# Moving VectorE's rotation of block one's q and k by a chunk, and reordering block two's feature chunks

## The reference

```python
def first_block(x, ...):                  # block one
    z = rmsnorm(x, g) @ w_in              # attention q, k, v | rwkv columns | gates
    q, k = rope(z_q), rope(z_k)           # 3 groups x 4 heads x 64, rotated
    o_attn = dilated_attention(q, k, v)
    o_rwkv = rwkv7_time_mix(z_rwkv)       # a recurrence, done here as chains of small products
    ...
def second_block(h, ...):                 # block two
    p = split(rmsnorm(h) @ w_in_2)        # q_a k_a v_a q_b k_b v_b q_idx k_idx w_idx q_c k_cmp v_cmp ...
    o_b = dsa(rope(q_b), rope(k_b), v_b, rope(q_idx), rope(k_idx), w_idx)
    o_c = nsa(rope(q_c), rope(k_cmp), v_cmp, rope(k_sel), v_sel, rope(k_win), v_win, ...)
    ...
def _compress(tok, pos_emb, w1, w2):      # of k_cmp and of v_cmp
    return gelu(blocks(tok + pos_emb) @ w1) @ w2
```

## Time and profile before

| what | value |
|---|---|
| time, median of 3 runs | 909.61 us (909.11 to 909.75) |
| the profiled execution: its own time | 909.91 us |
| its span, first to last instruction | 907.4 us |
| TensorE busy / VectorE busy / ScalarE busy | 882.2 / 606.8 / 480.5 us |
| mean granted TensorE clock | 0.998 of full |

### The profile page before, as it was taken

How to read it: one execution, slowest core, us unless ns; L and a number is a source line. 1 busy time by engine, 2 the same in 40 slices (tenths; PEclk the granted TensorE clock), 3 DMA queues, 4 the chain that set the end, 5 groups by cost and what they waited for, 6 DMA issues and landing times.

```text
span 907.4 us, 15435 instructions
## 1 busy us (share of the span) xinstructions
PE 882.2 (97%) x6552; PEld 748.8 (83%) x6552; DVE 606.8 (67%) x976; ACT 480.5 (53%) x775; POOL 29.2 (3%) x51
## 2 busy tenths in 40 slices
PE   7999999999899999999999999999999999999997
PEld 4999898787689888888889978776788788888885
DVE  4578978557856666656766577877863566666673
ACT  4775667436534444456444856484622545555561
POOL 0010000010000000000000020000000000000000
PEclk9999999999999999999999999999999999999999
DMA  9644333224468665555339764353817566665521
GB/s 336 190 140 140 99 119 114 63 83 150 178 248 282 188 190 190 200 202 187 121 112 229 164 210 144 111 186 107 277 38 206 146 187 188 191 193 194 199 95 47
DMA packets 131204, 150.71 MB, mean 166 GB/s; under 512 B 11808, under 2 KB 102176, under 8 KB 131008
## 3 DMA queue, kind: packets, MB, share of 16 engines
q1 hardware_dynamic: 129920, 145.57, 51.8%
q10 hardware_dynamic: 1216, 4.16, 1.2%
HBM read 148.67 MB, written 1.05 MB: 165 GB/s over the span
## 4 chain that ended last, share of the span: by engine, by line
PE 85%; DVE 7%; ACT 4%; issue 2%; DMA 1%; POOL 0%; POOLq 0%; ACTq 0%; DVEq 0%
PE psum L821 12%; PE psum L716 9%; PE psum L718 9%; PE psum L717 9%; PE psum L826 7%; PE psum L774 4%; PE psum L794 3%; PE psum L795 3%; PE psum L803 3%; PE psum L722 3%; PE psum L870 2%; PE psum L880 2%; PE psum L871 2%; PE psum L827 2%; DVE parts L2705 2%
## 5 line engine op out<-in xcount | busy, mean ns | idle before, releaser
L1808 ACT ACTIVATE parts<-low 128x1024 fp32r<-128x1024 f32 (+3 forms) x252 | 254.3, 1044 | 65.6 <-PE psum L718 48.3
L2705 DVE TENSOR_TENSOR parts<-low,parts 128x1024 fp32r<-128x1024 f32 (+3 forms) x156 | 183.7, 1206 | 37.7 <-ACT parts L1808 37.5
L716 PE MATMUL psum<-parts 128*128 128x512 f32 (+2 forms) x424 | 169.1, 399 | 4.6 <-DVE parts L2705 2.5
L718 PE MATMUL psum<-parts 128*128 128x512 f32 (+2 forms) x424 | 163.5, 386 | 0.0
L717 PE MATMUL psum<-parts 128*128 128x512 f32 (+2 forms) x424 | 163.4, 385 | 0.0
L1808 ACT ACTIVATE high<-psum 128x512 f32<-128x512 f32 (+6 forms) x115 | 63.4, 560 | 134.2 <-PE psum L827 76.4
L821 PE MATMUL psum<-parts 128*128 128x512 f32 x462 | 116.8, 392 | 0.0
L716 PEld LDWEIGHTS psum<-parts 128*128 128x128 f32 x424 | 79.6, 188 | 26.3 <-DVE parts L2705 4.5
L821 PEld LDWEIGHTS psum<-parts 128*128 128x128 f32 x462 | 86.9, 188 | 16.9
L718 PEld LDWEIGHTS psum<-parts 128*128 128x128 f32 x424 | 79.6, 188 | 16.4
L717 PEld LDWEIGHTS psum<-parts 128*128 128x128 f32 x424 | 79.8, 188 | 13.9
(11 more groups left out here) (313 smaller groups left out, 1310.6 us busy)
## 6 DMA issues: line engine op xcount, KB each, us to landing
low<-in_w_in_dram SPq DMA_DIRECT2D x40, 1024.0 KB, 5.3
low<-in_w_ffn_in_dram SPq DMA_DIRECT2D x44, 512.0 KB, 5.2
low<-in_w_ff_in_dram SPq DMA_DIRECT2D x16, 1024.0 KB, 5.7
low<-in_w_ff_out_dram SPq DMA_DIRECT2D x16, 1024.0 KB, 4.8
low<-in_w_ffn_out_dram SPq DMA_DIRECT2D x11, 1024.0 KB, 5.0
low<-in_w_out_dram SPq DMA_DIRECT2D x8, 1024.0 KB, 5.2
low<-in_w_ple_gate_dram SPq DMA_DIRECT2D x4, 1024.0 KB, 5.0
low<-consts_dram ACTq DMA_DIRECT2D x1, 2078.0 KB, 9.0
```

Of the source, the lines that this page charges most:

```text
L716: mm(o, l[0], r[0], start, False)
L718: return mm(o, l[1], r[0], False, stop)
L1808: return e.activation(o, a, ACT.Copy)
L2705: tt(rslot3(n, nk, width)[:, r, 0:w], slot3(n, nk, width)[:, r, 0:w], st.hi3(j)[:, r, 0:w].bitcast(F32), ALU.subtract) \
```

## The change

There are five edits. (1) Block one: the rotations are given to chunks by a table. Chunk 1's step holds none, chunk 2's rotates chunk 0, chunk 3's rotates 1, chunk 4's rotates 2 and 3, chunk 5's rotates 4; `rope1(5)` stays in the first gate. The buffers `zs` are four, and ScalarE waits for the rotation four chunks back. (2) Block two: the gathered chunk is n = 2 and the short one n = 3; q_b, q_idx and q_c are n = 4 to 6. Waits on rotations name the new numbers, and the three key copies come behind chunk 4. (3) `ahead` is gone: every slot is split in the order of the chunks. (4) The token chunk of v writes banks 5 and 6. (5) The partial sums of `_compress` are added by one matmul per half with a constant that has a one wherever row and column agree modulo 32; the constants have 128 more columns.

```diff
+C_SEL = C_SINC + 256
+C_END = C_SEL + 128
...
+    c[:, C_SEL:C_SEL + 16] = r % 32 == s[:, 0:16]
...
-        rt1 = [view3(P + 9216 + 1024 * i, 2, 256) for i in range(2)]
+        rt1 = [view3(P + 8704 + 512 * i, 2, 256) for i in range(4)]
...
-        plan_2 = [([(0, 256, 0)], [128, 128]), ([(256, 256, 0)], [128, 128]), ([(768, 256, 0)], [128, 128]),
-                  ([(1152, 256, 0)], [128, 128]), ([(1476, 256, 0)], [128, 128]),
-                  ([(1024, 64, 0), (1408, 64, 64), (1860, 64, 128), (1988, 64, 192)], [128, 128]), ([(1732, 128, 0)], [128])]
+        plan_2 = [([(0, 256, 0)], [128, 128]), ([(256, 256, 0)], [128, 128]),
+                  ([(1024, 64, 0), (1408, 64, 64), (1860, 64, 128), (1988, 64, 192)], [128, 128]), ([(1732, 128, 0)], [128]),
+                  ([(768, 256, 0)], [128, 128]), ([(1152, 256, 0)], [128, 128]), ([(1476, 256, 0)], [128, 128])]
...
-                yield from token_range(st2, 5, 2, 464, lambda i: [main_act.at("vt2", i), main_dve.at("vt2", i)], nothing)
+                yield from token_range(st2, 5, 2, 464, lambda i: [main_act.at("vt2", i), main_dve.at("vt2", i)], nothing, (5, 6))
...
-                    for g in range(4):
-                        t = mm(p[:, 16 * h:16 * h + 16], hd[:, h, :], ident[:, 32 * g:32 * g + 16], g == 0, g == 3)
+                    t = mm(p[:, 16 * h:16 * h + 16], hd[:, h, :], const(C_SEL, 16), True, True)
...
-                    if n == 1 or n == 0 and not ahead(st, j + 1):
+                    if n < 2:
                         split(st, j + 1, (n,))
                     yield
                 q.wait_ge(*main_pe.at(st.tag, j, 1))
-                if ahead(st, j + 2):
-                    split(st, j + 2, (0,))
                 read()
...
-                if n >= (2 if tag == "qk" else 4):
-                    q.wait_ge(*rope_dve.at(tag, n - 2))
+                if n >= 4:
+                    q.wait_ge(*rope_dve.at(tag, n - (4 if tag == "qk" else 2)))
...
-                    if n == 6:
-                        q.wait_ge(*rope_dve.at("in2", 5))
+                    if n == 4:
+                        q.wait_ge(*rope_dve.at("in2", 2))
...
+            turned_at = ((), (), (0,), (1,), (2, 3), (4,))
...
-                    yield from feature_chunk(st1, QK_AT + n, [128, 128], (lambda n=n: rope1(n - 1)) if n else nothing, nothing)
+                    yield from feature_chunk(st1, QK_AT + n, [128, 128], lambda n=n: [rope1(m) for m in turned_at[n]], nothing)
...
-                q.wait_ge(*rope_dve.at("in2", 6))
+                q.wait_ge(*rope_dve.at("in2", 3))
                 for n in range(15):
```

More of the change, by code:

```diff
@@ L426, in rope_to @@
         def rope_to(n):
-            return RC[:, 6:10:3, :] if n == 5 else RC[:, 10:11, :] if n == 6 else RC[:, 2 * (n - 2):2 * (n - 2) + 2, :]
+            return RC[:, 6:10:3, :] if n == 2 else RC[:, 10:11, :] if n == 3 else RC[:, 2 * (n - 4):2 * (n - 4) + 2, :]
         vt = view3(P + 21760, 2, 660)
@@ L833, in wide_chunk, with token_range @@
                 yield
-            def token_range(st, j0, n, w, freed, late):
+            def token_range(st, j0, n, w, freed, late, banks=None):
                 nk = 8 // n
-                banks = [next(pg), next(pg)]
+                banks = banks or [next(pg), next(pg)]
                 for s in range(n):
@@ L1541, in scores @@
                     bank(b)
-                q.wait_ge(*rope_dve.at("in2", 5))
+                q.wait_ge(*rope_dve.at("in2", 6))
                 q.wait_ge(*key_act.at(2))
@@ L1626, in nsa @@
                     bank(b)
-                q.wait_ge(*rope_dve.at("in2", 4))
+                q.wait_ge(*rope_dve.at("in2", 6))
                 q.wait_ge(*cmp_act.at("kc"))
@@ L1872, in head @@
                             read(n)
-            def ahead(st, j):
-                return st.tag == "st2" and j == 5
             def feature_chunk(st, j, widths, read):
@@ L1884, in feature_chunk, with token_range @@
                 q.wait_ge(*main_pe.at(st.tag, j, 1))
-                if ahead(st, j + 2):
-                    split(st, j + 2, (0,))
                 read()
                 yield
-            def token_range(st, j0, n, read):
+            def token_range(st, j0, n, read, banks=None):
                 nk = 8 // n
-                banks = [next(pg), next(pg)]
+                banks = banks or [next(pg), next(pg)]
                 for s in range(n):
@@ L1895, in token_range @@
                         for r in range(nk // 2):
-                            if i == 0 and (r == 1 or r == 0 and not ahead(st, j0 + s + 1)):
+                            if i == 0 and r < 2:
                                 split(st, j0 + s + 1, (r,))
@@ L2000, in qkv @@
                     b = next(pg)
-                    yield from feature_chunk(st1, QK_AT + n, [128, 128], lambda: rope_read("qk", n, 2, b, rt1[n % 2], qk[:, 2 * n:2 * n + 2, :]))
+                    yield from feature_chunk(st1, QK_AT + n, [128, 128], lambda: rope_read("qk", n, 2, b, rt1[n % 4], qk[:, 2 * n:2 * n + 2, :]))
             def gate(r):
@@ L2363, in read2 @@
                 else:
-                    m = 1 if n == 6 else 2
+                    m = 1 if n == 3 else 2
                     rope_read("in2", n, m, b, rz2[n % 2][:, 0:m, :], rope_to(n))
@@ L2382, in main_b @@
                         copy(RC[half_rows[1], 6, :], RC[half_rows[0], 6, :]).then_inc(key_act.up(2), 1)
-                yield from token_range(st2, 5, 2, read_vt)
+                yield from token_range(st2, 5, 2, read_vt, (5, 6))
             turns.alone(main_b())
@@ L2742, in feature_chunk, with token_range @@
                 yield
-            def token_range(st, j0, n, read, late):
+            def token_range(st, j0, n, read, late, banks=None):
                 nk = 8 // n
-                banks = [next(pg), next(pg)]
+                banks = banks or [next(pg), next(pg)]
                 for s in range(n):
@@ L2810, in rope @@
                 tt(dst, dst, zs, ALU.add).then_inc(rope_dve.up(tag, n), 1)
+            turned_at = ((), (), (0,), (1,), (2, 3), (4,))
             def rope1(n):
-                rope("qk", n, 2, rt1[n % 2], qk[:, 2 * n:2 * n + 2, :], C_COS, C_SIN)
+                rope("qk", n, 2, rt1[n % 4], qk[:, 2 * n:2 * n + 2, :], C_COS, C_SIN)
             def qkv():
@@ L3291, in rope2 @@
                 if n >= 2:
-                    m = 1 if n == 6 else 2
-                    rope("in2", n, m, rz2[n % 2][:, 0:m, :], rope_to(n), *((C_COSC, C_SINC) if n == 6 else (C_COS, C_SIN)))
+                    m = 1 if n == 3 else 2
+                    rope("in2", n, m, rz2[n % 2][:, 0:m, :], rope_to(n), *((C_COSC, C_SINC) if n == 3 else (C_COS, C_SIN)))
             def read_vt(i, p):
                 if i == 0:
-                    q.wait_ge(*rope_dve.at("in2", 5))
+                    q.wait_ge(*rope_dve.at("in2", 2))
                     for m, half in enumerate(half_rows):
@@ L3310, in main_b @@
                     yield from feature_chunk(st2, n - 2, plan_2[n][1], lambda: rope2(n - 1), nothing)
-                yield from token_range(st2, 5, 2, read_vt, lambda: rope2(6))
+                yield from token_range(st2, 5, 2, read_vt, lambda: rope2(6), (5, 6))
             turns.alone(main_b())
```

2 lines of the change are left out of this document (removed).

## The result

The changed kernel is slower: 913.01 us, median of 11 runs (910.58 to 914.98), against 909.78 for the kernel before on the same chip (11 runs, 908.97 to 909.98). The ratio is 1.0038, 95% interval [1.0028, 1.0047]: about 3.5 us lost by the ratio, 3.2 by the two medians. The forecast of 909.2 missed, and so did its range, which ended at 911.2. The profiled execution took 913.07 us with a span of 911.1, 3.7 us longer than before; what follows is read from this one execution.

A forecast was written before the change was run, and what follows sets the result against it. TensorE, busy 97% of the span, was taken as the bound, so only its waits counted. Block one -1.5, block two +1.1, the rest 0 gave -0.4 us: 909.5 profiled, median 0.3 lower, 909.2 us; range 906.6 to 911.2.

The forecast's parts named there:

- Edit 1, forecast 1.5 us: Block one, level 1: masks start before the rotation, TensorE's waits of 1.04 and 0.16 us go; gain 1.5 us.
- VectorE's cover at level 4: Block one: the moved rotation's 1.93 us fits VectorE's 2.62 us idle before level 4's masks, leaving 0.7 us; no cost.
- if another operand of level 1 is late too; none shows: Block one, level 1: condition under which edit 1's gain would fall to its lower bound, nothing.
- The walk through `main_b`: Block two: ScalarE's list order makes new TensorE waits of 4.94 us against 3.84 us removed; loss 1.1 us.
- the bounds of the sum: Block two: from a gain of 3.84 us without new waits to 2.6 us more loss if q_b's slot lands late.
- Edit 5, forecast nothing: Line 1607: 1.28 us less matmul time on TensorE, given back at the wait at 567.74 us; counted as nothing.
- The forecast wait of 1.7 us: TensorE's wait at 567.74 us, ended by a VectorE split, grows from 0.4 to 1.7 us.
- The late slot: Rival, block two: q_b's load lands at 504.8 us, its start slips 2.6 us more; 911.8 us, chance 8 in 100.
- The bank alone: Rival, end of `main_b`: v's own banks remove 1.40 us and no wait replaces it; 906.7 us, chance 8 in 100.

The follow-up runs named there:

- the filled pause: Changed kernel with 20 extra matmuls of 256 columns, adding no result, in TensorE's pause behind the short chunk: 909.86 us, ratio 1.0008.
- e11_changed_splits_first: Changed kernel in its own chunk order, each slot split before the ended chunk is read, bank 3 for q_b: 910.16 us, ratio 1.0012.
- e6_splits_first: Kernel before with its own chunk order, v in banks 5 and 6, v's slots split before the readings, key copies after: 907.33 us, ratio 0.9980.
- With the load held: Changed kernel with one gate load held until the small products of `nsa_keys` are done: 912.25 us, ratio 1.0029.
- order alone: Kernel before with edits 2 to 4 only (block two's chunk order, earlier splits undone, v in banks 5 and 6): 913.66 us, ratio 1.0048.
- half-filled: Changed kernel with 10 extra matmuls of 256 columns, adding no result, in the pause behind the short chunk: 910.18 us, ratio 1.0006.
- the kernel before and the held load: Kernel before with one gate load held until the small products of `nsa_keys` are done: 909.72 us, ratio 1.0004.

## Why the prediction was wrong

Point by point, on the profiled executions.

- **Edit 1, forecast 1.5 us: the mechanism right, the size wrong.** The wait went and VectorE's cover at level 4 held (0.40 us left, 0.7 forecast). Kept were 0.55 us in this pair of executions. The failed step is "if another operand of level 1 is late too; none shows": what came next was no operand of the products but their code. In both executions one 16 KB page of code arrives between 104.2 and 105.3 us; before, that lay ahead of the end of the wait for the masks, and now it lies within the products, and TensorE reaches the edge of its code sooner (0.28 us "issue" at 106.70, 0.26 at 117.62). In the burst TensorE went on 1.4 us after the page's transfer had ended (548.57, then 549.95); 1.4 us after 105.25 is 106.65, and it went on at 106.70. Seven of the nine profiled kernels with edit 1 have this pause, ended 1.2 to 1.5 us behind that page, and the six with a pause in the burst went on 1.3 to 1.5 us behind theirs. This is read from the rows; no run here takes the page away in block one, so it is not shown as the burst's is.
- **The walk through `main_b`, forecast +1.1: right.** Pauses of 2.67, 1.11 and 0.55 us in the view, forecast about 2.5, 0.9 and 0.5; none at v's first slot. `main_b` lost 2.33 us, 1.37 of which the filled pause shows to be the clock; the 0.96 is what that leaves.
- **The missing term: the half clock, 1.37 us.** The step that failed is the one that lets a pause cost what it lasts. The trace of before shows the clock at 1.00 through all its pauses there, up to 1.49 us, so nothing in it priced a fall; the bounds of the sum had no place for one.
- **The second missing term: 1.90 us in the burst of `nsa_keys`.** The prediction looked for waits on engines and slots, and counted loads only for the slot that they fill. The load that pushed the page was not part of the change; it only shifted against TensorE.
- **Edit 5, forecast nothing: right.** It stayed nothing in all pairs of runs that differ by it, within what these can tell. The forecast wait of 1.7 us came as two, 0.40 and 0.82 us.
- **The rivals.** The late slot did not happen in the changed kernel (the pause was ScalarE's list), but the slot landed at most 0.5 us before ScalarE wanted it (501.2, then 501.64), and in `e11_changed_splits_first` it was the bound. "The bank alone" was wrong as put: other waits came in place of the bank's. What banks 5 and 6 are worth with the old order and the old splits, no run shows; with the splits ahead of the readings (`e6_splits_first`) the waits at v are gone.

The sum by what was measured: -0.55 + 0.96 + 1.37 + 1.90 + 0 = +3.68 us, against -0.4 forecast. It closes on one pair of executions; how many of the eleven runs of the changed kernel had the half clock and the late page, their times do not tell.

The Trainium skill, "Runtime: NRT & Kernel Launch", section Instruction fetch mechanics, says that crossing a page of code costs little, since it is mostly hidden. The trace of before agrees at the burst (no pause at 544.65); the changed kernel does not (1.52 us).

What stays open: why the page comes ahead of that load's data in the kernel before, and behind them in the kernels with a pause in the burst. The instructions ahead of the burst are as many in both, and the load is released by the same chunk. With the load held the page still began only 1.7 us ahead of the burst (544.62, then 546.34), before it was 3.0 (541.63, then 544.65): the load delays it, and something else had made it later too. Also open is what decides whether the clock falls: with the pauses of the kernel before it stayed up in that kernel and in the run with edit 5 alone, and fell in two other runs.

## What to carry to other kernels

A pause of TensorE is not priced by its length alone: where a change makes one longer than any in the profile, give the half clock behind it a term, from nothing to what a fall costs (here 1.37 to 2.55 us). In dense runs of small products treat the code page as one more operand: a load issued just ahead of the run can hold it up, and to hold that load until the run is over cost nothing measurable here. Where one in-order engine both reads the finished bank and prepares the next operand, put the preparing first before reordering the work.

## What the runs showed of the hardware

- TensorE's clock fell to half at single pauses of 2.67 us (changed kernel, order alone), 2.22 (splits first in the changed order) and 1.78 us (half-filled, in that execution): soon behind them, or, with the order alone, before the pause was over (0.71 from 504 to 505 us, first product at 505.15). In the run with edit 1 alone it fell too, to 0.67 and 0.50 from 522 to 526 us, behind two pauses of 1.23 and 0.64 us close together, and with the kernel before and the held load to 0.50 from 524 to 526 us, behind 1.24 and 0.64; in the kernel before the same pauses left it at 1.00. There a fall cost little: v's second slot was waited for anyway, and that wait had shrunk to nothing.
- A 16 KB page of TensorE's code, 0.9 us on its own, began at 544.62 us with the gate load held and at 547.54 without: about 3 us later, behind 1 MB of weights. The Trainium skill, "DMA: Bandwidth & Descriptors", section Queues, rings and completion order, says that a DMA engine takes turns between its queues packet by packet. By that rule the page would have come soon after its request. The trace does not show the request, but it does not look like that rule: the load's data ran from 544.2 to 547.8 us, and the page began among the last of them.
